# Splitting fp32 weights for TensorE in pairs of batches: one 1024-column split in place of two 512-column ones

## The chip, the core and the metric

One Trainium2 chip, one of its cores. The metric is the device time of one execution in microseconds (us), the median of several. All inputs are float32, and so is the output.

## What is computed

Two decoder blocks in a row over 256 tokens with model width 2048. Cut to what matters here:

```python
def first_block(x, ...):
    proj = rms_norm(x, g_mix_pre) @ w_in              # 2048 x 9728
    y_attn = sliding_window_attention(...)            # 16 heads of 64
    o = hgrn2_recurrence(...)                         # 8 heads of 128, a gated linear recurrence
    merged = sigmoid(gate_a) * (y_attn @ w_attn_branch) + sigmoid(gate_b) * (y_hgrn @ w_hgrn_branch)
    x = x + rms_norm(merged @ w_out)
    x = x + rms_norm((silu(gate) * up) @ w_down)      # gate, up = h @ w_gate_up, width 5632
    x = x + rms_norm((p @ w_ple_proj) * sigmoid(h @ w_ple_gate))

def second_block(x, ...):
    proj = rmsnorm(x) @ w_in_2
    o_a = dsa_mixer(...)                              # top-k index, latent attention, 8 heads
    o_b = fox_mixer(...)                              # forgetting attention, 8 heads
    x = x + concat(o_a, o_b) @ w_o
    x = x + conv_ffn(rmsnorm(x), w_up, conv_w, conv_b, w_down)
    return rmsnorm(x)
```

The weights, some 480 MB, are read once. Each product with a weight is made of three TensorE products of halves: a float32 number is split into a part `hi` that TensorE's fp32r format holds and a rest `lo`, and hi*hi + hi*lo + lo*hi is summed in PSUM.

## The kernel before, in words

The host packs the weights of all phases into units of 8 tiles of 128x128, so 128 partitions x 1024 columns, 512 KB. There are 902 units in one stream, in the order in which TensorE uses them. Half a unit, 4 tiles or 512 columns, is a batch; there are 1804, and a **tick** is the place of one batch in the program. All engines walk over the same ticks:

- **SyncE** (`fetch`, L2510) brings unit u into `raw`, a ring of 4 units (`RAW`), once the rest of unit u-4 has been taken (signal `rest`).
- **ScalarE (ACT)** (`half(b)`, L1071) casts batch b to `hi`, a ring of 6 batches (`SPL`). It waits until TensorE has finished batch b-6 (signal `gemm`, key "batch"), whose slot it takes.
- **VectorE (DVE)** (`low_half(b)`, L1637) subtracts: `lo` = `raw` - `hi`, in a ring of 6 too. It waits for `half(b)` (signal `halved`) and for the same batch of TensorE.
- **TensorE (PE)** (L609 to 1045) takes `hi` and `lo` of its batch, all through the helper `mm` at L613/614.

At tick t ACT and DVE split batch t+5 (`LOOK`). Beside that each engine has an `Agenda` (L311): a generator per piece of work (a group's epilogue, an attention head, a step of the recurrence) that names the ticks of its steps. Each engine executes strictly in the program's order. The loops of ACT (L1599) and DVE (L2431) are:

```python
for tick in range(plan.ticks):
    if tick in URGENT:
        agenda.run(tick)
    if tick + LOOK < plan.ticks:
        low_half(tick + LOOK)
```

From tick 48 on every tick is in `URGENT`, so the agenda of a tick comes ahead of the split made in it (ACT has three ticks as exceptions, `SPLIT_FIRST`). The agenda of tick t+1 comes behind it.

Groups come in two kinds. In the one the weight is what is loaded, and a batch is 4 matmuls of 512 columns with `hi` and 4 of 256 with `lo`. In a **quarter** (`batch_of_quarter`, L1011) the activations are loaded and the weights stream, 512 columns at a time, into two banks m = 0 and 1: six matmuls a batch. In the last three batches of a quarter (`SKEW`) TensorE does m=0 for all three first, and m=1 for all three after it, and a batch is finished for `gemm` only with m=1. So those three batches end one behind the other, about 2 us later than their m=0 halves.

The places outside the stream that matter for the prediction:

- **The ladder of the recurrence** (`hgrn`, PE L746, ACT L1463, DVE L2213), once for each of two sets of heads, from tick HG = 121 and from tick 193 (L588). It has 9 stages n = 0 to 8, four ticks apart (`LEVEL`). `product(n)` on DVE stands at tick HG+1+4n (n from 2 on), the copy of the keys (L1471) on ACT at HG+2+4n (n = 1 to 7), the matmuls `sums(n)` on PE at HG+4+4n, and `place(n)` on DVE at HG+6+4n (L604 to 606). `product(n+1)` needs `sums(n)`; the keys' copy needs `product`; `sums` need both.
- Its end: PE transposes at `HG_TURN` and `HG_TURN`+2 (L807, ticks 275 and 277), ACT and DVE make `HS` from the first at tick 276 (L1495, L1630), and the second pair of transposes needs those banks.
- **Latent attention** (`latent`, L851, L1506, L2341), two chains of four heads, 14 ticks a head, the one at odd ticks and the other at even ones, and **forgetting attention** (`forget`, L883, L1528, L2366), four chains of two heads. ACT lays the transposed probabilities (L1520, L1542) shortly ahead of the product that needs them.
- The crossings between phases (`CROSS`, L538): PE transposes `X` chunk by chunk (L653), ACT and DVE make `XS` from it, and the first batches of the next phase need it.

Of the kernel before, what the change touches and what calls it, by code (L numbers as in the profile page):

```python
# [8 lines left out]
F32 = mybir.dt.float32  # L9
# [3 lines left out]
ALU = mybir.AluOpType  # L13
# [11 lines left out]
RAW = 4  # L25
BT = 4
BW = BT * P
SPL = 6
LOOK = 5

PIECES = [(0, 1), (1, 2)] + [(c, c + 2) for c in range(2, 16, 2)]
# [297 lines left out]
def program(nc, d, out):  # L329
# [4 lines left out]
    with ctx:  # L334
        def sb(name, shape, dt=F32):
            return ctx.enter_context(nc.sbuf_tensor(name, shape, dt))
# [3 lines left out]
        def signal(name, step=1):  # L340
            signals.append(Signal(ctx.enter_context(nc.semaphore(name)), step))
            return signals[-1]

        raw = sb("raw", [P, RAW, UW])
        hi = sb("hi", [P, SPL, BW], F32R)
        lo = sb("lo", [P, SPL, BW], F32R)
        X = sb("X", [P, NC, T])
# [30 lines left out]
        def const(name, a=0, b=None, rows=slice(0, P)):  # L378
            lo_, hi_ = CCOL[name]
            return cst[rows, lo_ + a:(hi_ if b is None else lo_ + b)]  # L380
# [12 lines left out]
        def sums_of(n):  # L393
            a = 12 * BY_TOKEN.index(n) + 8
            return cols[:, a:a + 2]
# [4 lines left out]

        def cut(q, n=QUARTER):
            return slice(n * q, n * q + n)

        ident = const("ident")
        ones = const("ones", 0, P)
# [88 lines left out]
        halved, rest, gemm = signal("halved"), signal("rest"), signal("gemm")  # L494
# [114 lines left out]
        def tensor(eng, counting=False):  # L609
# [3 lines left out]
            def mm(o, l, r, start, stop):  # L613
                return eng.matmul(o, l, r, start=start, stop=stop, skip_group_check=True)  # L614

            def clear(k):
                for signal_key in free.get(k, ()):
                    on.wait_ge(*signal_key)
# [332 lines left out]
            def high(b, pos, g, j):  # L951

                w = hi[:, b % SPL, pos * P:(pos + 1) * P]
                if j == 0:
# [11 lines left out]
            def low_part(b, pos, g, j):  # L966

                w = lo[:, b % SPL, pos * P:(pos + 1) * P]
                o = bank[g.bank]
# [18 lines left out]
            def with_high(g, k, b, m):  # L988
# [4 lines left out]
                if k == 0:  # L993
                    clear(g.banks[m])
                o, w = bank[g.banks[m]], hi[:, b % SPL, :]
                mm(o, x[:, m * P:(m + 1) * P], w, k == 0, False)
                mm(o, x[:, T + m * P:T + (m + 1) * P], w, False, False)

            def with_low(g, k, b, m):

                x = operand(g, g.tiles[BT * k][2])[0]
                last = k == g.n // BT - 1
                t = mm(bank[g.banks[m]], x[:, m * P:(m + 1) * P], lo[:, b % SPL, :], False, last)
                done = [("batch", b)] if m else []
# [63 lines left out]
        def scalar(eng, counting=False):  # L1068
            on, agenda = On(eng, counting), Agenda()

            def half(b):  # L1071
                u, part = b // (UT // BT), b % (UT // BT)
                on.wait_ge(*((in_raw[u % RAW], u) if b else (in_first, 0)))
                if b >= SPL:
                    on.wait_ge(gemm, ("batch", b - SPL))
                eng.copy(hi[:, b % SPL, :], raw[:, u % RAW, part * BW:(part + 1) * BW]).then_inc(halved.next(b), 1)  # L1076
# [41 lines left out]
            def quarter_of_values(g):  # L1118

                n = ROOT_OF[g.kind]  # L1120
                if g.kind == "hi":
                    o = hh[g.q]["v"].rearrange("p (t n) -> p t n", t=2)
                else:
                    on.wait_ge(i_dve, "sel")
                    o = b_bv[:, :, cut(g.q)]
                on.wait_ge(n_dve, (n, "root"))
                for m in range(2):
                    if m:
                        yield 1
                    on.wait_ge(gemm, ("half", g.g, m))  # L1130
                    eng.activation(o[:, m, :], bank[g.banks[m]], ACT.Identity, scale=roots_of(n)[:, m:m + 1]).then_inc(
                        t_act.next((g.g, m)), 1)
# [17 lines left out]
            def quarter_of_gates(g):  # L1150

                o = {"ga": XT, "hg": h_gate[g.q % 2], "gb": gated}[g.kind]
                if g.kind == "gb":
                    on.wait_ge(h_pe, (0, "turned", 1))
                elif g.kind == "hg":
                    on.wait_ge(h_dve, (g.q, "product", 2))
                on.wait_ge(n_dve, ("mix", "root"))
                for m in range(2):
                    if m:
                        yield 1  # L1160
                    on.wait_ge(gemm, ("half", g.g, m))
                    eng.activation(o[:, m, :] if g.kind == "hg" else o[:, m, cut(g.q)], bank[g.banks[m]], ACT.Sigmoid, scale=roots_of("mix")[:, m:m + 1]).then_inc(
                        t_act.next((g.g, m)), 1)
# [35 lines left out]
            def quarter_of_down1(g):  # L1199
                q, p = g.i  # L1200
                if g is by["down1", (3, 2)]:
                    return
                for m in range(2):
                    if m:
                        yield 1
                    if p == 0:
                        on.wait_ge(gemm, ("half", g.g, m))
                        eng.copy(Y[:, m, cut(q)], bank[g.banks[m]]).then_inc(t_act.next((g.g, m)), 1)
                    elif p == 2:
                        square_of_down(g, m)  # L1210
# [376 lines left out]
            def enter_first(c):  # L1587
                on.wait_ge(in_x[piece_of(c)], 0)
                eng.activation(XS[:, c, 0:T], X[:, c, :], ACT.Identity, scale=col("g_mix_pre", c)).then_inc(
                    upper.next(("mix", c)), 1)  # L1590
# [4 lines left out]
            eng.activation(sums_of("final"), prm[:, 0:2], ACT.Identity).then_inc(n_act.next("first table"), 1)  # L1595
            for b in range(LOOK):
                enter_first(b)
                half(b)
            for tick in range(plan.ticks):  # L1599
                first = tick in URGENT and tick not in SPLIT_FIRST  # L1600
                if first:
                    agenda.run(tick)
                if tick + LOOK < plan.ticks:
                    half(tick + LOOK)
                if tick + LOOK < NC:
                    enter_first(tick + LOOK)
                if tick == NORM_AT["mix"]:
# [15 lines left out]
        def vector(eng, counting=False):  # L1623
            on, agenda = On(eng, counting), Agenda()

            def tt(o, a, b, op):
                return eng.tensor_tensor(o, a, b, op)  # L1627
# [9 lines left out]
            def low_half(b):  # L1637
                u, part = b // (UT // BT), b % (UT // BT)
                on.wait_ge(halved, b)
                if b >= SPL:  # L1640
                    on.wait_ge(gemm, ("batch", b - SPL))
                tt(lo[:, b % SPL, :], raw[:, u % RAW, part * BW:(part + 1) * BW], hi[:, b % SPL, :].bitcast(F32),
                   ALU.subtract).then_inc(rest.next(b), 1)
# [779 lines left out]
            def enter_first(c):  # L2423
                lower(XS[:, c, :], X[:, c, :], ("mix", c), col("g_mix_pre", c))

            eng.memset(HS[:, 0, :].bitcast(F32), 0.0).then_inc(zeros.next(0), 1)
            on.wait_ge(in_pre, 0)
            for b in range(LOOK):
                enter_first(b)
                low_half(b)  # L2430
# [281 lines left out]
```

## Time and profile before

| | |
|---|---|
| median of 3 runs | 2654.79 us (2652.17 to 2655.65) |
| span of the profiled execution | 2653.3 us |
| its busy time, PE | 2636.2 us, 99% |
| its busy time, PE loading weights | 2236.2 us, 84% |
| its busy time, DVE | 1871.7 us, 71% |
| its busy time, ACT | 1510.4 us, 57% |
| weights and inputs read | 488.44 MB, 186 GB/s |

For the profiled execution only its span is given, from its first to its last instruction; it lies 1.5 us under the median of the runs, inside their spread. Engines are named as in the profile: PE is TensorE's matmuls, PEld its weight loads, DVE VectorE, ACT ScalarE, POOL GpSimd, SP SyncE. Times inside the profile count from the span's start. A matmul's end in it is modelled, and matmuls overlap in their tails, as do neighbouring instructions of ACT and DVE by up to 0.1 us.

### The profile page before, as it was taken

What the parts mean: (1) busy time and instruction counts of PE and PEld (TensorE: products, weight loads), DVE (VectorE), ACT (ScalarE), POOL (GpSimd) and SP (SyncE); (2) the same over time, 40 slices, a digit from 0 to 9 for tenths busy, and PEclk for the clock granted to TensorE, in tenths of its full rate; (3) what the DMA queues carried; (4) which work ended last, traced back from release to release, by engine and by line L of the source; (5) the groups of instructions that cost most, each with busy time, mean ns of one, the idle gap of its engine ahead of it and who ended that gap; (6) DMA issues with size and microseconds to landing.
All of it is one profiled execution on the core that took longest, in us unless ns stands there. A gap on an engine that the chain in (4) does not pass through costs nothing.

```text
span 2653.3 us, 38713 instructions
## 1 busy us (share of the span) xinstructions
PE 2636.2 (99%) x13730; PEld 2236.2 (84%) x13730; DVE 1871.7 (71%) x3539; ACT 1510.4 (57%) x3006; POOL 38.8 (1%) x56
## 2 busy tenths in 40 slices
PE   9999999999999999999999999999999999999998
PEld 7888888888888888888887888988888888888887
DVE  7877566465876577657767678666688758866885
ACT  7775555455655455545557665554566546655654
POOL 0000000000000000000003000000000000000000
PEclk9999999999999999999999999999999999999999
DMA  8455547666666666665665555545656666666565
GB/s 282 147 167 162 181 152 238 192 208 197 184 187 191 206 204 187 193 191 186 188 188 178 173 161 187 156 149 162 186 180 192 193 192 186 190 190 192 187 192 160
DMA packets 136817, 493.09 MB, mean 186 GB/s; under 512 B 15704, under 2 KB 16216, under 8 KB 135856
## 3 DMA queue, kind: packets, MB, share of 16 engines
q1 hardware_dynamic: 134064, 480.04, 57.8%
q0 software_dynamic: 2272, 10.31, 1.2%
q8 instruction: 109, 1.79, 0.3%
q14 instruction: 84, 0.69, 0.1%
q10 hardware_dynamic: 288, 0.26, 0.0%
HBM read 488.44 MB, written 4.21 MB: 186 GB/s over the span
## 4 chain that ended last, share of the span: by engine, by line
PE 98%; DVE 1%; ACT 0%; issue 0%; DMA 0%; DVEq 0%; SPq 0%; ACTq 0%
PE bank L614 97%; PE bank L653 0%; DVE lo L1627 0%; DVE X L1630 0%; PE bank L729 0%; DVE arena L1627 0%; DVE XS L1630 0%; DMA raw<-in_ws_mix 0%; ACT sq_t L1181 0%; PE bank L867 0%; PE bank L901 0%; ACT hi L1076 0%; PE bank L677 0%; PE bank L694 0%; PE bank L807 0%
## 5 line engine op out<-in xcount | busy, mean ns | idle before, releaser
L1627 DVE TENSOR_TENSOR lo<-raw,hi 128x512 fp32r<-128x512 f32 x1804 | 1233.2, 690 | 659.7 <-ACT hi L1076 548.2
L1076 ACT CAST hi<-raw 128x512 fp32r<-128x512 f32 x1804 | 1098.0, 619 | 696.8 <-PE bank L614 678.1
L614 PE MATMUL bank<-XS,hi 128*128 128x512 f32 x3632 | 1000.2, 396 | 1.6 <-DVE XS L1630 1.6
L614 PEld LDWEIGHTS bank<-XS,hi 128*128 128x128 f32 x3632 | 620.8, 189 | 90.8 <-issue 4.0
L614 PEld LDWEIGHTS bank<-XS,lo 128*128 128x128 f32 x3632 | 557.0, 189 | 77.1
L614 PE MATMUL bank<-XS,lo 128*128 128x256 f32 x3632 | 578.5, 281 | 0.0
L614 PE MATMUL bank<-hi,HS 128*128 128x512 f32 x1952 | 545.6, 391 | 0.0
L614 PE MATMUL bank<-hi,XS 128*128 128x512 f32 x1600 | 448.3, 394 | 1.7 <-DVE XS L1630 1.1
L614 PEld LDWEIGHTS bank<-hi,HS 128*128 128x128 f32 x1952 | 364.0, 188 | 75.5 <-ACT hi L1076 1.3
L614 PEld LDWEIGHTS bank<-hi,XS 128*128 128x128 f32 x1600 | 296.8, 189 | 66.0 <-ACT hi L1076 4.4
L614 PE MATMUL bank<-lo,HS 128*128 128x512 f32 x976 | 321.6, 389 | 0.0
L614 PE MATMUL bank<-lo,XS 128*128 128x512 f32 x800 | 259.4, 390 | 0.0
L614 PEld LDWEIGHTS bank<-lo,HS 128*128 128x128 f32 x976 | 183.2, 188 | 38.8 <-DVE lo L1627 0.4
L614 PEld LDWEIGHTS bank<-lo,XS 128*128 128x128 f32 x800 | 150.5, 188 | 32.0
L1082 ACT COPY tmp_t<-bank 128x256 f32<-128x256 f32 x235 | 86.6, 373 | 143.7 <-PE bank L614 143.5
L1627 DVE TENSOR_TENSOR u_t<-bank,tmp_t 128x256 f32<-128x256 f32 x208 | 87.7, 423 | 51.2 <-ACT tmp_t L1082 50.9
L1630 DVE SCALAR_TENSOR_TENSOR u_t<-u_t,prm 128x255 f32<-128x255 f32 (+1 forms) x176 | 84.8, 483 | 9.0
L1627 DVE TENSOR_TENSOR u_t<-u_t,r_t 128x256 f32<-128x256 f32 x200 | 84.8, 424 | 6.8
L614 PE MATMUL bank<-arena 128*128 128x128 f32 (+4 forms) x672 | 87.4, 299 | 0.0
L614 PEld LDWEIGHTS bank<-arena 128*128 128x128 f32 (+2 forms) x672 | 71.7, 182 | 8.6 <-issue 2.4
L1285 ACT ACTIVATE u_t<-u_t,prm 128x256 f32<-128x256 f32 x88 | 53.0, 602 | 44.8 <-DVE u_t L1627 44.8
L1627 DVE TENSOR_TENSOR u_t<-u_t 128x256 f32<-128x256 f32 x178 | 75.3, 423 | 2.6 <-ACT u_t L1148 0.8
(198 smaller groups left out, 985.5 us busy)
## 6 DMA issues: line engine op xcount, KB each, us to landing
raw<-in_ws_ffn SPq DMA_DIRECT2D x528, 512.0 KB, 3.5
raw<-in_ws_mix SPq DMA_DIRECT2D x338, 512.0 KB, 3.6
raw<-in_ws_ple SPq DMA_DIRECT2D x35, 512.0 KB, 4.1
arena<-in_gains POOLq DMA_DIRECT2D x4, 1024.0 KB, 5.9
X<-in_xt POOLq DMA_DIRECT2D x1, 2048.0 KB, 13.1
t5rows<-t5row POOLq DMA_DIRECT2D x8, 256.0 KB, 5.1
out<-arena SPq DMA_DIRECT2D x8, 256.0 KB, 2.5
X<-in_x SPq DMA_DIRECT2D x7, 256.0 KB, 5.3
```

Source lines behind the costliest of these rows:

```text
L614: return eng.matmul(o, l, r, start=start, stop=stop, skip_group_check=True)
L1076: eng.copy(hi[:, b % SPL, :], raw[:, u % RAW, part * BW:(part + 1) * BW]).then_inc(halved.next(b), 1)
L1082: eng.copy(low(g), bank[g.bank][:, T:2 * T]).then_inc(copied.next(g.g), 1)
L1285: eng.activation(v, tile(g.u[0]), ACT.Identity, scale=col("cw", 176 + j), bias=col("cb", j)).then_inc(curved.next((g.g, "v")), 1)
L1627: return eng.tensor_tensor(o, a, b, op)
L1630: return eng.scalar_tensor_tensor(out=o, in0=a, scalar=s, in1=b, op0=op0, op1=op1)
```

## The change

From batch 8 on the two batches of a unit are split by one instruction on ACT and one on DVE, of 1024 columns instead of 512, into two neighbouring slots of the rings. That happens where the even one of the two had its turn; where the odd one had, nothing is left. The wait is the later one of the two: for batch b+1-6 = b-5, since the second of the two slots is written as well. Both batches get the same count of `halved` and of `rest`, so a waiter that has seen the even one waits no more for the odd one. The size of the rings, the order of TensorE and all agendas stay.

```diff
@@ -26,6 +26,7 @@
 SPL = 6
+PAIRED = 8
 LOOK = 5
@@ -401,6 +402,9 @@
+        def pair_of(ring, b):
+            return ring[:, b % SPL:b % SPL + 2, :].rearrange("p b n -> p (b n)")
+
@@ -1071,6 +1075,11 @@
             def half(b):
                 u, part = b // (UT // BT), b % (UT // BT)
                 on.wait_ge(*((in_raw[u % RAW], u) if b else (in_first, 0)))
+                if b >= PAIRED:
+                    if part == 0:
+                        on.wait_ge(gemm, ("batch", b + 1 - SPL))
+                        eng.copy(pair_of(hi, b), raw[:, u % RAW, :]).then_inc(halved.next(b, b + 1), 1)
+                    return
                 if b >= SPL:
                     on.wait_ge(gemm, ("batch", b - SPL))
@@ -1637,6 +1646,12 @@
             def low_half(b):
                 u, part = b // (UT // BT), b % (UT // BT)
                 on.wait_ge(halved, b)
+                if b >= PAIRED:
+                    if part == 0:
+                        on.wait_ge(gemm, ("batch", b + 1 - SPL))
+                        tt(pair_of(lo, b), raw[:, u % RAW, :], pair_of(hi, b).bitcast(F32), ALU.subtract).then_inc(
+                            rest.next(b, b + 1), 1)
+                    return
                 if b >= SPL:
                     on.wait_ge(gemm, ("batch", b - SPL))
```

How the order moves, at two places. The first is DVE in the second ladder, from `place(3)` at tick 211 over `product(5)` (the five `arena<-arena`, tick 214) to `place(4)` at tick 215. Before:

```order
L2268 COPY_PREDICATED arena<-lvl,bank 128x4x16x4 x2
L1627 TENSOR_TENSOR lo<-raw,hi 128x512 x3
L1627 TENSOR_TENSOR arena<-arena 128x4x8x8 x4
L1627 TENSOR_TENSOR arena<-arena 128x64
L1627 TENSOR_TENSOR lo<-raw,hi 128x512
L1627 TENSOR_TENSOR X<-X,bank 128x512
L2268 COPY_PREDICATED arena<-lvl,bank 128x4x8x8 x2
```

With the change (its lines are numbered higher, and `lo` is 1024 wide):

```order
L2283 COPY_PREDICATED arena<-lvl,bank 128x4x16x4 x2
L1636 TENSOR_TENSOR lo<-raw,hi 128x1024 x2
L1636 TENSOR_TENSOR arena<-arena 128x4x8x8 x4
L1636 TENSOR_TENSOR arena<-arena 128x64
L1636 TENSOR_TENSOR X<-X,bank 128x512
L2283 COPY_PREDICATED arena<-lvl,bank 128x4x8x8 x2
```

Ahead of the product there stood the subtraction of batch 218, which waits for batch 212; now there stands that of 218 and 219, which waits for batch 213. The subtraction that stood behind the product is gone.

The second place is ACT in the same ladder, from the keys of `sums(4)` (tick 211) over those of `sums(5)` (tick 215) to those of `sums(6)` (tick 219). Before:

```order
L1471 COPY arena<-arena 128x32x8 x2
L1076 CAST hi<-raw 128x512 x4
L1471 COPY arena<-arena 128x16x16 x2
L1076 CAST hi<-raw 128x512 x4
L1471 COPY arena<-arena 128x8x32 x2
```

With the change:

```order
L1480 COPY arena<-arena 128x32x8 x2
L1081 CAST hi<-raw 128x1024 x2
L1480 COPY arena<-arena 128x16x16 x2
L1081 CAST hi<-raw 128x1024 x2
L1480 COPY arena<-arena 128x8x32 x2
```

The four casts of batches 216 to 219 had four ticks for their turns, 211 to 214; the two wide ones stand at ticks 211 and 213, and the second waits for batch 213. Nothing stands any more between it and the keys of tick 215.

## Rows read from the trace of the kernel before

**Rows 1.** The page: span; busy time, share and instructions of each engine.

```profile
span 2653.3 us, 38713 instructions
...
PE 2636.2 (99%) x13730; PEld 2236.2 (84%) x13730; DVE 1871.7 (71%) x3539; ACT 1510.4 (57%) x3006; POOL 38.8 (1%) x56
```

**Rows 2.** Groups by form: count, busy us, mean ns, idle before and its releasers.

```profile
L1627 DVE TENSOR_TENSOR lo<-raw,hi 128x512 fp32r<-128x512 f32 x1804 | 1233.2, 690 | 659.7 <-ACT hi L1076 548.2 <-PE bank L614 96.9
L1076 ACT CAST hi<-raw 128x512 fp32r<-128x512 f32 x1804 | 1098.0, 619 | 696.8 <-PE bank L614 678.1 <-DMA raw<-in_ws_mix 13.2 <-issue 0.3
...
L1276 ACT CAST HS<-u_t 128x256 fp32r<-128x256 f32 x44 | 18.0, 408 | 60.2 <-DVE u_t L1627 60.2
...
L1627 DVE TENSOR_TENSOR arena<-arena 128x1024 f32<-128x1024 f32 x2 | 2.4, 1218 | 0.0
```

**Rows 3.** All waits: engine, line, releaser: us in total, times, longest.

```profile
PEld bank L614 <- ACT hi L1076: 9.1, 18, 1.1
```

**Rows 4.** Timeline, one batch after another in a plain stretch: start, us, instruction.

```profile
1000.55 1.09 PE L614 MATMUL bank<-XS,hi 128*128 128x512 f32 x4
...
1001.96 1.09 PE L614 MATMUL bank<-XS,hi 128*128 128x512 f32 x4
```

**Rows 5.** Timeline, second ladder, ticks 209 to 213.

```profile
336.16 1.06 PE L614 MATMUL bank<-arena 128*128 128x128 f32 x8
...
338.30 1.62 DVE L1627 TENSOR_TENSOR arena<-arena 128x256 f32<-128x256 f32 x5
...
338.64 0.62 ACT L1076 CAST hi<-raw 128x512 fp32r<-128x512 f32 x1 [1.06 <-PE bank L614]
...
339.96 0.71 ACT L1471 COPY arena<-arena 128x256 f32<-128x256 f32 x2 [0.70 <-DVE arena L1627]
...
342.55 1.06 PE L614 MATMUL bank<-arena 128*128 128x128 f32 x8
```

**Rows 6.** Timeline, the same ladder at a quarter's end, ticks 213 to 217.

```profile
344.06 1.56 DVE L1627 TENSOR_TENSOR arena<-arena 128x256 f32<-128x256 f32 x5
...
346.39 0.62 ACT L1076 CAST hi<-raw 128x512 fp32r<-128x512 f32 x1 [2.97 <-PE bank L614]
...
346.91 0.71 ACT L1471 COPY arena<-arena 128x256 f32<-128x256 f32 x2
...
348.92 1.06 PE L614 MATMUL bank<-arena 128*128 128x128 f32 x8
```

**Rows 7.** Timeline, the ladder's end, ticks 276 and 277.

```profile
436.66 1.40 DVE L1630 SCALAR_TENSOR_TENSOR HS<-bank,prm,HS 128x512 fp32r<-128x512 f32 x2
...
437.31 0.63 ACT L1076 CAST hi<-raw 128x512 fp32r<-128x512 f32 x1 [0.41 <-PE bank L614]
...
438.47 1.03 PE L807 MATMUL bank<-cst,arena 128*128 128x128 f32 x8
```

**Rows 8.** Timeline, one head of latent attention at even ticks.

```profile
1718.02 0.37 ACT L1082 COPY tmp_t<-bank 128x256 f32<-128x256 f32 x1 [1.05 <-PE bank L614]
...
1718.29 0.49 ACT L1520 COPY arena<-bank 128x384 f32<-128x384 f32 x1
...
1719.22 0.83 PE L614 MATMUL bank<-arena 128*128 128x128 f32 x6
```

**Rows 9.** Timeline, forgetting attention.

```profile
1782.69 0.88 ACT L1542 COPY arena<-bank 128x384 f32<-128x384 f32 x2
...
1784.09 0.61 PE L614 MATMUL bank<-arena 128*128 128x128 f32 x4
```

**Rows 10.** Timeline, a crossing behind a quarter of `o1`, ahead of the second feed-forward network.

```profile
1874.36 0.39 PE L614 MATMUL bank<-lo,HS 128*128 128x512 f32 x1
...
1875.89 0.68 DVE L1627 TENSOR_TENSOR X<-X,bank 128x512 f32<-128x512 f32 x1
...
1877.31 0.38 PE L653 MATMUL bank<-cst,X 128*128 128x128 f32 x2
```

**Rows 11.** The page: DMA issues, count, KB each, us from issue to landing.

```profile
raw<-in_ws_ffn SPq DMA_DIRECT2D x528, 512.0 KB, 3.5
```

## Prediction

> **What bounds the kernel now.** First the page's busy times: of a span of 2653.3 us PE is busy 2636.2, and only 17.1 are left [rows 1]. So the bound is TensorE, and an edit can take away at most those 17.1 us unless it makes PE do less. This one doesn't: order and number of its 13730 matmuls stay. Then the groups: the two splits are the largest work of ACT (1098.0 us) and DVE (1233.2), but both engines stand idle in front of them, ACT for 678.1 us until PE gives a slot free, DVE for 548.2 us until ACT has cast [rows 2]. They are ahead and wait. Then the waits: PE's loads waited for `hi` 9.1 us in all, in 18 places [rows 3]. Faster splits can return little more than that. What the change can cost is read from the other side, the chains in which PE waits for a step of ACT or DVE that stands in the same queue as the splits, and for those I read the timeline.
>
> **What it removes.** From batch 8 on 1796 batches become 898 pairs. On DVE two of 690 ns become one of 1218 ns, which the trace has in another place [rows 2]. On ACT no cast of 1024 columns is there; 256 columns take 408 ns and 512 take 619 [rows 2], so 211 ns more for 256 columns, and 619 + 2 x 211 = 1041 ns. Two casts of 619 bound it from above (1.24 us); from below I have no nearer row than the slope itself, and the price of a single cast, 0.62, as the extreme. I take 1.04. So DVE saves 162 ns and ACT 197 ns a pair, 145 and 177 us in all, on engines that are 71% and 57% busy, ahead of PE and waiting. On the path this is worth about nothing; it hides behind PE's matmuls and would count only where the splits are late, in the 9.1 us of rows 3. The 2 x 898 waits that PE no longer has to make are worth nothing either: batches follow each other every 1.41 us [rows 4] with both waits in them. Nothing in these rows tells a satisfied wait from none; were it 10 ns, 1796 would be 18 us, which is the gain's outer bound and more than PE's idle time.
>
> The Trainium skill, page "Perfetto Trace Analysis", section "Optimizing Scalar/DVE Operations", says that grouping into larger operations helps if the engine is saturated, and that where these engines aren't saturated but cause bubbles on others, breaking instructions up may let work be done sooner. By that rule this change goes the wrong way; rows 2, with hundreds of microseconds of idle time ahead of the splits, are the second case.
>
> **What it adds: later splits.** Before, batch b could be split once batch b-6 was done, five batches or 7.0 us ahead of its use, and was ready 0.62 + 0.69 us after that; 5.7 us were left. Now the even batch of a pair starts one batch later, 5.6 us ahead, and needs 1.04 + 1.22 = 2.26; 3.4 us are left. That covers the splits themselves nearly everywhere. The fetch of a unit waits for the second subtraction as before, whose slot is the same; it comes 2.26 - 1.31 = 0.95 us later, of about 11 us (eight batches) between slot and next use, with a landing of 3.5 us [rows 11]. Nothing.
>
> **What it moves: every step at an even tick.** The wide split stands at odd tick t and waits for the end of batch t itself, not t-1. All that ACT has at tick t+1 now starts no earlier than 1.04 us after batch t, and all that DVE has there 2.29 us after it (cast, 0.03 to pass on, subtraction). Before, ACT's was free at the end of batch t-1 plus 0.62. Behind that waiting instruction the agenda of the even tick is queued, and PE waits for it where its slack is smaller. Place by place:
>
> - *The ladders.* `product` is at an even tick in both (HG = 121 and 193, +1+4n). At tick 209 the cast that waits for batch 209 starts at 338.64; the product then already runs on DVE, from 338.30, and the keys are done at 340.67, 1.9 us ahead of the sums at 342.55 [rows 5]. Now: cast 338.64 to 339.68, subtraction 339.71 to 340.93, product (1.62, of which 0.1 overlaps) to 342.45, keys (0.71) to 343.2. The sums come 0.65 us late. Of the steps with keys behind a `sums` (`product` 2 to 7, six a ladder, 12 in all) four have their odd tick at the third last batch of a quarter, whose end is put off behind the m=0 halves: ticks 141, 205, 213, 221. There the cast waits until 346.39 [rows 6]: then cast to 347.43, subtraction to 348.68, product (1.56) to 350.15, keys to 350.9, against sums at 348.92, 2.0 us late. The delay comes again in each step, since the gate is counted from PE's own progress: 8 x 0.65 + 4 x 2.0 = **13.2 us**. `product(8)` needs no keys and comes just in time.
> - *The ladder's end.* Cast 437.31 to 438.35, subtraction to 439.60, then the two `HS` of 1.40 to 441.0; PE wants their banks at 438.47 and half a microsecond later [rows 7]: **2.0 us**. It happens once, with the banks of the first set of heads.
> - *Latent attention.* The chain at even ticks has four heads. ACT's copies begin when the batch is done, 1718.02, and end at 1718.78, 0.44 us ahead of PE at 1719.22 [rows 8]. Behind a wide cast they end 1.05 later: 0.6 us, four times, **2.4 us**.
> - *Forgetting attention.* The same at two places with 0.52 us of slack (1783.57 to 1784.09) [rows 9]: 2 x 0.5 = **1.0 us**.
> - *Crossings behind `o1`.* The quarter's last batch ends at 1874.75; cast to 1875.82, subtraction to 1877.05, the addition at the even tick (0.68) to 1877.7, against 1877.31 [rows 10]: 0.4 us in each of four quarters, **1.6 us**.
> - *Where splits were late already.* The start, the second half of `wa`, and the three phase changes with chains of DVE: even batches come up to 0.95 us later there. I take one such delay for each of these five, **5 us**. This is an estimate from the 0.95, without a row of its own; zero and 10 us are its ends.
>
> Sum: 13.2 + 2.0 + 2.4 + 1.0 + 1.6 + 5 = 25.2 us. Against the span of 2653.3 that is 2678.5; the median of the runs lies 1.5 us higher than the profiled span, so **2680 us**. With a wide cast of 1.24 us each of the some 30 places would be 0.2 later, 6 us more.
>
> **The rivals.** (1) *The rings absorb it*: the cast or DVE's queue is not what holds the products, or my place of the gate is off, and PE's stalls stay under 0.2%, which is 5.3 us and about what a measurement of this kernel can tell from no change. For it: 3.4 us stay in hand nearly everywhere. Against it: the ladder's chain has its own slack of 1.9 us, not the ring's. Time: 2655 (2650 to 2660). Chance 0.10. (2) *Faster*, the other side: the splits that PE waited for become 0.2 us a pair shorter on ACT and 0.16 on DVE, and where ACT is behind by several batches the queue drains sooner. It decides from the point at which those savings outweigh the waits for the later slot, so if most of the 9.1 us of rows 3 are ACT's backlog and the ladders stay in time. It gives back at most 9.1, likely half: 2650. Chance 0.05. The skill's first clause, on grouping, is this case. (3) *The delays chain*: a late product delays DVE's `place` and the next subtraction, the keys delay the next wide cast, and PE's stalls in ladder and attention double, or its clock falls in one of them: 25 x 2 = 50 us, 2705. For it: DVE is at 71% on average and more in the ladder. Chance 0.12. (4) The change does what it says; the order shows the moved instructions, so I give that no chance of its own.
>
> **How the numbers follow.** The forecast, slower by 6 to 42 us, has 0.73. Its own range: the ladders alone at half price give 2662, all places at full price with a 1.24 us cast and 10 us for the late splits 2692; knock-on between them brings it to 2698. The range that holds 8 in 10 leaves out rivals 1 and 2 and the larger part of 3: 2662 to 2700. Faster by over 0.2% only in rival 2, 0.05; within 0.2% rival 1, 0.10; slower 0.85.
>
> **What would show it.** Right: DVE `lo` at 1.22 us and ACT `hi` at 1.04, 898 of each; PE's idle time up from 17 to some 42 us, half of it ahead of the `arena` matmuls of L614 in the two ladders, in stalls of 0.6 and of 2 us with ACT L1471's copy as releaser; some 2 us at L807; the matmuls' own durations unchanged. Wrong: sums in time with the keys done ahead of them, PE's new idle time in front of `hi` and `lo` of plain batches (then the ring is the bound and not the ladder), or a shorter batch than 1.41 us, which would mean that a wait cost PE something.

## The result, and the profile after

The changed kernel takes **2717.97 us** (median of 4 runs, 2712.19 to 2720.03), the kernel before beside it on the same chip 2654.67 (4 runs). The ratio is 1.0234, with a 95% interval of 1.0221 to 1.0246: slower by 63.3 us in the medians and by 61.7 us in the profiled spans (2715.0 against 2653.3), some 62 us below. The forecast was 2680 in a range of 2662 to 2700. Direction and kind of loss were right, its size was not. One of the 11 runs of `plain_only` below took 2884.18 us at a mean granted clock of 0.849 of 2.4 GHz, where the others on record had 0.994 to 0.999, and is left out of its comparison.

First the page of the changed kernel: span, and busy time, share and instructions of each engine; then the two split groups (count, busy us and mean ns, idle before and its releasers). Line numbers are those of each kernel's own file: L1636, L1081, L1480, L618 here are L1627, L1076, L1471, L614 of the kernel before. `arena` is a shared area of SBUF in which several phases keep their tiles.

```profile
span 2715.0 us, 35753 instructions
...
PE 2656.9 (98%) x13730; PEld 2239.8 (82%) x13730; DVE 1765.1 (65%) x2641; ACT 1368.5 (50%) x2108; POOL 40.9 (2%) x56
...
L1636 DVE TENSOR_TENSOR lo<-raw,hi 128x1024 fp32r<-128x1024 f32 x898 | 1099.7, 1226 | 811.8 <-ACT hi L1081 796.8 <-PE bank L618 11.2
...
L1081 ACT CAST hi<-raw 128x1024 fp32r<-128x1024 f32 x898 | 937.5, 1046 | 801.0 <-PE bank L618 794.6 <-DMA raw<-in_ws_mix 5.3
```

Against [rows 1, 2]: the wide splits cost what they were put at, 1226 and 1046 ns. ACT does 142 us less and DVE 107 us less than before, a fifth to a quarter less than the 177 and 145 that the prediction counted, and both stand idle longer ahead of the splits. PE's idle time is 2715.0 - 2656.9 = 58.1 us, where it was 17.1; the other 20.7 us are in its busy time, and come back below.

What PE's matmuls wait for, from all waits of the changed kernel (engine, line, releaser: us in total, times, longest):

```profile
PE bank L618 <- ACT arena L1480: 13.9, 11, 2.2
PE bank L657 <- DVE X L1639: 7.5, 4, 3.2
PE bank L618 <- DVE X L1636: 3.3, 5, 1.0
PE bank L618 <- DVE XS L1639: 3.0, 6, 0.7
PE bank L618 <- ACT hi L1081: 2.6, 4, 1.1
PE bank L657 <- DVE X L1636: 2.4, 3, 0.8
PE bank L681 <- DVE arena L1636: 2.2, 3, 0.8
PE bank L811 <- DVE HS L1639: 1.8, 1, 1.8
PE bank L618 <- ACT arena L1121: 1.7, 1, 1.7
```

And, of what its weight loads wait for, the splits:

```profile
PEld bank L618 <- DVE lo L1636: 6.5, 12, 1.2
...
PEld bank L618 <- ACT hi L1081: 4.7, 7, 1.6
```

The largest is the one that the prediction named: the ladders' sums (L618) behind the keys (ACT L1480), 11 stalls. The others are spread over steps of many kinds, `X`, `XS`, `HS`, and copies of the attention. The splits themselves hold PE a little more than before: its loads wait for `lo` 6.5 us, for `hi` 4.7 and for the eight narrow casts at the start 2.3, together 13.5, against 9.5 before (9.1 of [rows 3] and 0.4 for `lo`); its matmuls, which the loads overlap, wait 5.0 us for them against 0.4. To see every place, not only waits that have a releaser, I paired each matmul of PE with the same one of the kernel before, whose order is the same, and took by how much its start had moved at the ends of each stretch. The table gives these growths in us; a gain is negative, the columns behind `after` are the experiments below, and a dash is no row of the forecast.

| place | forecast | after | odd_turn | ladder_only | no_ladder | narrow_early | act_only |
|---|---|---|---|---|---|---|---|
| start and first attention | part of 5 | 12.6 | -0.1 | 1.3 | 12.4 | 7.4 | 7.5 |
| two ladders | 13.2 | 20.0 | 0.2 | 22.3 | 0 | 6.1 | 11.4 |
| second half of `wa` | part of 5 | 1.7 | 3.4 | 0 | 1.7 | 0.4 | 1.4 |
| ladder's end | 2.0 | 2.7 | 0 | 0 | 2.2 | 1.2 | 1.7 |
| merges of heads | - | 4.4 | 0 | 0 | 3.3 | 0 | 1.4 |
| four phase changes | part of 5 | 11.5 | 11.5 | 1.4 | 11.2 | 2.7 | 7.8 |
| keys and values, latent attention | 2.4 | 4.9 | 0.8 | 0 | 4.8 | 0.6 | 3.3 |
| forgetting attention | 1.0 | 0.4 | -1.5 | -1.7 | 0.3 | -1.7 | 0 |
| crossings behind `o1` | 1.6 | 4.0 | 1.1 | 0 | 4.0 | 0 | 2.7 |
| second feed-forward network | 0 | 0.0 | 18.4 | 0 | 0 | 0 | 0 |
| sum | 25.2 | 61.8 | 33.7 | 23.3 | 40.0 | 16.9 | 37.1 |

(What is missing to a sum lies in small steps between the places. The forecast's 5 us counted three phase changes, of the four that there are. Of the 4.4 us at the merges in `after`, 1.1 lie with a fall of the clock at 475.7, told below, and not with a stall.) One ladder step in the timeline of the changed kernel, a product whose odd tick is a quarter's third last batch; its sums are those that start at 336.16 in [rows 5] (start, us, instruction, in brackets the idle time before and its releaser):

```profile
356.75 1.05 ACT L1081 CAST hi<-raw 128x1024 fp32r<-128x1024 f32 x1 [3.21 <-PE bank L618]
...
357.83 1.23 DVE L1636 TENSOR_TENSOR lo<-raw,hi 128x1024 fp32r<-128x1024 f32 x1 [3.03 <-ACT hi L1081]
...
358.97 1.76 DVE L1636 TENSOR_TENSOR arena<-arena 128x256 f32<-128x256 f32 x5
...
360.76 0.71 ACT L1480 COPY arena<-arena 128x256 f32<-128x256 f32 x2 [2.38 <-DVE arena L1636]
...
361.61 1.13 PE L618 MATMUL bank<-arena 128*128 128x128 f32 x8 [2.24 <-ACT arena L1480]
```

Here stand the links that the prediction drew out of [rows 5, 6]: ACT and DVE each idle 3 us in front of a split whose slot isn't free, then cast, subtraction, product, keys, one behind the other, and PE waits 2.24 us at the sums. In [rows 6], a place of the same kind, the keys were done at 347.62, 1.3 us ahead of the sums.

The place that the prediction had no line for is the first attention. Before, where ACT's copy L1112 is the last thing PE waits for:

```profile
61.88 0.58 ACT L1112 COPY arena<-bank 128x512 f32<-128x512 f32 x1
...
62.55 0.93 PE L614 MATMUL bank<-arena 64*128 64x128 f32 x8
```

And in the changed kernel:

```profile
66.17 1.04 ACT L1081 CAST hi<-raw 128x1024 fp32r<-128x1024 f32 x1 [1.20 <-PE bank L618]
...
67.12 0.58 ACT L1121 COPY arena<-bank 128x512 f32<-128x512 f32 x1
...
67.75 0.93 PE L618 MATMUL bank<-arena 64*128 64x128 f32 x8 [1.68 <-ACT arena L1121]
```

Before, the copy ended at 62.46 and PE followed at 62.55, with 0.09 us in hand. Whatever stands ahead of that copy in ACT's queue shows at PE nearly in full. In this stretch there are 14 stalls of over 0.35 us, which sum to 10.2. In one of them, of 1.3 us at 146.53, PE waits for a cast itself; but that cast stood behind steps of ACT of which the first had waited 3.62 us for DVE, whose steps stood behind a wide subtraction.

### The profile page after: what moved, and what is told of

The parts are those of the page before. It is cut to its first block, busy times and chain, and to the rows that moved or that the text cites. A ratio compares the mean times of both kernels' runs of the same rounds, so it can differ in the third digit from the quotient of the medians.

```text
span 2715.0 us, 35753 instructions
## 1 busy us (share of the span) xinstructions
PE 2656.9 (98%) x13730; PEld 2239.8 (82%) x13730; DVE 1765.1 (65%) x2641; ACT 1368.5 (50%) x2108; POOL 40.9 (2%) x56
## 3 DMA queue, kind: packets, MB, share of 16 engines
q8 instruction: 109, 1.79, 0.3%
## 4 chain that ended last, share of the span: by engine, by line
PE 87%; DVE 6%; ACT 4%; issue 2%; DMA 1%; ACTq 0%; SPq 0%; DVEq 0%
PE bank L618 86%; ACT hi L1081 2%; DVE lo L1636 2%; DVE arena L1636 1%; PE bank L657 1%; DMA raw<-in_ws_mix 1%; DVE u_t L1636 0%; DVE arena L1639 0%; DVE X L1636 0%; ACT arena L1459 0%; ACT sq_t L1190 0%; DVE X L1639 0%; ACT arena L1480 0%; DVE arena L1643 0%; DVE XS L1639 0%
## 5 line engine op out<-in xcount | busy, mean ns | idle before, releaser
L1636 DVE TENSOR_TENSOR lo<-raw,hi 128x1024 fp32r<-128x1024 f32 (+1 forms) x906 | 1105.1, 1221 | 814.2 <-ACT hi L1081 796.8
L1081 ACT CAST hi<-raw 128x1024 fp32r<-128x1024 f32 x898 | 937.5, 1046 | 801.0 <-PE bank L618 794.6
L618 PE MATMUL bank<-XS,hi 128*128 128x512 f32 x3632 | 1001.0, 397 | 3.1 <-DVE XS L1639 1.2
L618 PEld LDWEIGHTS bank<-XS,hi 128*128 128x128 f32 x3632 | 621.4, 189 | 92.5 <-issue 6.0
L618 PEld LDWEIGHTS bank<-XS,lo 128*128 128x128 f32 x3632 | 556.7, 189 | 80.7 <-DVE lo L1636 3.7
L618 PE MATMUL bank<-XS,lo 128*128 128x256 f32 x3632 | 579.4, 281 | 1.1 <-DVE lo L1636 0.9
L618 PE MATMUL bank<-hi,HS 128*128 128x512 f32 x1952 | 548.2, 392 | 0.7 <-ACT hi L1081 0.7
L618 PE MATMUL bank<-hi,XS 128*128 128x512 f32 x1600 | 449.5, 395 | 3.9 <-DVE XS L1639 1.8
L618 PEld LDWEIGHTS bank<-hi,HS 128*128 128x128 f32 x1952 | 365.5, 189 | 76.7 <-ACT hi L1081 1.4
L618 PEld LDWEIGHTS bank<-hi,XS 128*128 128x128 f32 x1600 | 297.2, 189 | 69.4 <-issue 5.3
L618 PE MATMUL bank<-lo,HS 128*128 128x512 f32 x976 | 322.9, 391 | 0.6 <-DVE lo L1636 0.5
L618 PE MATMUL bank<-lo,XS 128*128 128x512 f32 x800 | 259.8, 391 | 0.1
L618 PEld LDWEIGHTS bank<-lo,HS 128*128 128x128 f32 x976 | 184.1, 189 | 40.1 <-DVE lo L1636 1.5
L618 PEld LDWEIGHTS bank<-lo,XS 128*128 128x128 f32 x800 | 150.4, 188 | 33.2 <-DVE lo L1636 1.3
L1639 DVE SCALAR_TENSOR_TENSOR u_t<-u_t,prm 128x255 f32<-128x255 f32 (+1 forms) x176 | 84.9, 483 | 59.5 <-ACT u_t L1294 56.4
L618 PE MATMUL bank<-arena 128*128 128x128 f32 (+4 forms) x672 | 89.8, 303 | 19.6 <-ACT arena L1480 13.9
L618 PEld LDWEIGHTS bank<-arena 128*128 128x128 f32 (+2 forms) x672 | 71.2, 184 | 33.8 <-DVE arena L1636 11.9
L1636 DVE TENSOR_TENSOR u_t<-u_t 128x256 f32<-128x256 f32 x178 | 75.4, 424 | 30.1 <-ACT u_t L1157 23.9
L1636 DVE TENSOR_TENSOR u_t<-u_t,r_t 128x256 f32<-128x256 f32 x200 | 85.0, 425 | 6.7
L1636 DVE TENSOR_TENSOR u_t<-bank,tmp_t 128x256 f32<-128x256 f32 x208 | 86.6, 417 | 0.0
```

What stands on the lines that cost most here:

```text
L1081: eng.copy(pair_of(hi, b), raw[:, u % RAW, :]).then_inc(halved.next(b, b + 1), 1)
L1639: return eng.scalar_tensor_tensor(out=o, in0=a, scalar=s, in1=b, op0=op0, op1=op1)
```

## The experiments

Two theories. **A**: the loss is in the queues. A wide split waits in front of steps that PE needs, and they run after it. **B**: the loss is in the rings. The splits of plain batches come too late for PE, because a pair is begun later and takes longer. I name the runs as their texts do; B there is in some of them a cost of each pair, spread evenly over the run. The kernel before took 2655.65 us (median of 7 runs) beside the first four experiments and 2655.22 (21 runs) beside the others; differences are against these. Code is shown in part.

### odd_turn: the same wide splits, at the odd batch's turn

The wait is for the same batch, but the split now stands one tick later, behind the agenda of the even tick instead of ahead of it.

```diff
                 if b >= PAIRED:
-                    if part == 0:
-                        on.wait_ge(gemm, ("batch", b + 1 - SPL))
-                        eng.copy(pair_of(hi, b), raw[:, u % RAW, :]).then_inc(halved.next(b, b + 1), 1)
+                    if part == 1:
+                        on.wait_ge(gemm, ("batch", b - SPL))
+                        eng.copy(pair_of(hi, b - 1), raw[:, u % RAW, :]).then_inc(halved.next(b - 1, b), 1)
                     return
```

(and the same in `low_half`; the waits for `raw` and for `halved` stand at the odd turn too.)

> The same 898 wide splits with the same gate (pair (b-1, b) waits for batch b-6), but standing at the odd batch's turn, one tick later in the program: behind the agenda of the even tick instead of ahead of it. Theory A (what costs is the queue: the even tick's steps stand behind an instruction that waits for the batch of its own tick): the steps at even ticks are free again, PE's stalls in the two ladders fall from 16 us to under 3, and the whole comes to 2655 to 2668 us. Theory B (the ring is what costs: even batches are split one batch later and 1.04 + 1.22 us long, whatever the order): gate and width are unchanged, so the time stays near 2715.

Measured: 2687.72 us (2686.44 to 2688.83), ratio 1.0121 [1.0105, 1.0136]. About half of the loss is gone, which neither theory had. The table says why. In start and attention, ladders, ladder's end, merges, and keys, values and latent attention the growth falls from 44.6 us to 0.9, with splits just as wide and the same slots to wait for: for these places A is shown. But the phase changes lose 11.5 us again (how, comes below), and the second feed-forward network, which had lost nothing, now loses 18.4. Its waits in 2100 to 2500 us of this kernel:

```profile
ACT u_t L1295 <- DVE u_t L1637: 38.5, 38, 1.2
ACT HS L1307 <- DVE u_t L1637: 38.2, 20, 2.0
ACT u_t L1301 <- DVE u_t L1640: 31.9, 21, 1.7
PEld bank L618 <- DVE lo L1637: 11.6, 25, 0.5
```

And of the kernel before in the same stretch, where the list has no wait of PE for `lo`:

```profile
ACT HS L1297 <- DVE u_t L1627: 21.4, 21, 1.0
ACT u_t L1285 <- DVE u_t L1627: 18.6, 43, 0.4
ACT u_t L1291 <- DVE u_t L1630: 13.7, 22, 0.6
```

ACT's own steps on `u_t` wait for DVE, whose steps stand behind wide subtractions. The cast at the odd turn stands behind those waiting steps, as in this piece of `odd_turn`'s timeline:

```profile
2202.04 1.23 DVE L1637 TENSOR_TENSOR lo<-raw,hi 128x1024 fp32r<-128x1024 f32 x1
...
2204.27 0.42 ACT L1301 ACTIVATE u_t<-u_t 128x256 f32<-128x256 f32 x1 [1.66 <-DVE u_t L1640]
...
2204.59 1.03 ACT L1082 CAST hi<-raw 128x1024 fp32r<-128x1024 f32 x1
```

and the subtraction reaches PE late: 25 waits of its loads in this stretch, none over 0.5 us. PE's late splits are what B names, but what makes them late is again the queue, whose order puts the split last. So one order hurts the steps, the other the splits.

### ladder_only and no_ladder: where the loss lies

Both take the change's own form, in `ladder_only` only where the even turn lies in the ticks of the two ladders, in `no_ladder` everywhere else (there the test is `not any(...)`); this is `ladder_only`'s edit:

```diff
+LADDERS = [(121, 160), (193, 232)]
+
+
+def paired(b):
+    turn = b - b % 2 - LOOK
+    return b >= PAIRED and any(x <= turn < y for x, y in LADDERS)
...
-                if b >= PAIRED:
+                if paired(b):
```

> Pairs only where their turn lies in one of the two ladders (ticks 121 to 159 and 193 to 231), narrow splits elsewhere: 78 of 1804 ticks. Theory A (PE stalls at chains with little slack): the ladder's 11 stalls of 0.8 to 2.4 us come back in full, +15.7 us and a little in small ones, 2668 to 2674. Theory B (a cost per pair, spread over the run): 4% of the loss of 63 us, +3, 2658.

> The complement: pairs everywhere but in the two ladders. Theory A: 63 - 17 = +46 us, 2701, and PE's stalls ahead of the arena matmuls fed by the keys' copy are gone. If the stalls of the different places hide one another, more than that: 2705 to 2715. Theory B: +60, 2715.

Measured: `ladder_only` 2677.08 us (2675.12 to 2678.47), ratio 1.0078 [1.0062, 1.0095]; `no_ladder` 2694.9 (2693.03 to 2697.4), 1.0148 [1.0133, 1.0164]. That is 21.4 and 39.2 us, together 60.6: the ladders and the rest add up, and don't feed each other. 78 ticks of 1804 hold a third of the loss, at the sums, as PE's waits in `ladder_only` show:

```profile
PE bank L624 <- ACT arena L1486: 14.5, 12, 2.2
```

A cost spread evenly over the pairs, B in that run's text with 2658, falls as the cause of that third. But two thirds lie outside the ladders, where the forecast had 12 us.

### narrow_early: both splits at the even turn, but narrow

```diff
-                        on.wait_ge(gemm, ("batch", b + 1 - SPL))
-                        eng.copy(pair_of(hi, b), raw[:, u % RAW, :]).then_inc(halved.next(b, b + 1), 1)
+                        for k in range(2):
+                            on.wait_ge(gemm, ("batch", b + k - SPL))
+                            eng.copy(hi[:, (b + k) % SPL, :], raw[:, u % RAW, k * BW:(k + 1) * BW]).then_inc(halved.next(b + k), 1)
```

(and the same in `low_half`, which waits for each batch's `halved` too.)

> The order of the change with instructions of the old width: both batches of a pair are split at the even one's turn, each by its own 512-column cast and subtraction with its own gate (b-6, then b-5). Steps at even ticks now wait for the own tick's batch, but for 0.62 + 0.69 = 1.3 us behind it and not 2.3. Theory A: an ordinary step of the ladder is 0.3 us in time again, the four at a quarter's end are 1.0 us late, other places lose 0.4 (ACT) or 0.95 us (DVE) less each: in all +15 to +25 us, 2670 to 2680. If the width is what costs: no change against before, 2655. If the order is all: near 2715.

Measured: 2672.94 us (2671.84 to 2675.04), ratio 1.0066 [1.0051, 1.0081]; 17.3 us. The queues' order and the last wait are those of the change; what is left behind that wait is 0.62 and 0.69 us instead of 1.05 and 1.23. The same ladder place as above in its timeline:

```profile
344.39 1.76 DVE L1637 TENSOR_TENSOR arena<-arena 128x256 f32<-128x256 f32 x5
...
346.19 0.71 ACT L1481 COPY arena<-arena 128x256 f32<-128x256 f32 x2 [1.85 <-DVE arena L1637]
...
347.04 1.13 PE L618 MATMUL bank<-arena 128*128 128x128 f32 x8 [1.23 <-ACT arena L1481]
```

A stall of 1.23 us where the wide split made 2.24, though the two narrow subtractions together take longer than the wide one. So of the 62 us some 17 come with the moved wait alone, and 45 are that after it the whole pair has to be done before anything behind it.

### act_only: wide on ACT alone

The block `if b >= PAIRED` in `low_half` is taken out, and DVE subtracts batch by batch as before.

> ACT's cast wide at the even turn as in the change, DVE's subtractions narrow in their own turns. Theory A: the product of the ladder starts 0.53 us earlier, behind a subtraction of 0.69 instead of 1.22, so ordinary steps are 0.1 to 0.6 us late instead of 0.8 to 1.3 and those at a quarter's end 1.5; steps of ACT at even ticks lose the full 1.05 us. In all +30 to +45 us, 2685 to 2700. If DVE's width were the whole cost: 2655 to 2665; if ACT's were: 2715.

Measured: 2692.5 us (2690.91 to 2693.02), ratio 1.0139 [1.0126, 1.0153]; 37.3 us. ACT's wide cast alone makes 37 of the 62 us, and DVE's wide subtraction on top of it the other 25: a step passes through both queues. The subtraction wide by itself was not run, so 25 is its part behind a wide cast only. In the ladders, whose chain runs over DVE, act_only has 11.4 of 20 us.

### plain_only and hybrid: wide where no step is near

`turn_of` gives the turn of the pair, even (0), odd (1), or None for narrow ones. For `plain_only` the list holds only the two feed-forward networks; for `hybrid` it adds the other stretches and takes the odd turn everywhere but in the last:

```diff
+WIDE = [(0, 236, 1), (256, 425, 1), (470, 950, 1), (1070, 1235, 1), (1330, 1804, 0)]
+
+
+def turn_of(b):
+    even = b - b % 2 - LOOK
+    if b < PAIRED:
+        return None
+    return next((part for x, y, part in WIDE if x <= even < y), None)
```

with `[(470, 950, 0), (1330, 1804, 0)]` in `plain_only`.

> Pairs as in the change, but only in the plain stretches of the two feed-forward networks (turns at ticks 470 to 949 and 1330 to 1803): 477 of 898 pairs, none at a chain that PE waits for. Theory A (the cost sits in chains with little slack, and the saved time of ACT and DVE buys nothing): 2655, within 0.1% of before, though ACT's and DVE's busy time falls by some 90 us each. A cost per pair: 477/898 of 62 us, +33. A gain per pair from shorter instructions: below 2650.

> Pairs in 85% of the ticks, each stretch in the order that left PE alone there: at the odd batch's turn in the attention, ladders, merges and the heads of the second block, at the even one's turn in the second feed-forward network, narrow splits at the phase changes and at wa. Theory A (order and slack of each place, additive): 2652 to 2657, the loss of 62 us gone with 763 pairs still there. If pairs cost something by themselves that order doesn't mend, or if odd and even turns disturb each other: over 2665.

Measured: `plain_only` 2654.48 us (2653.15 to 2655.71), ratio 0.9997 [0.9988, 1.0006]; `hybrid` 2655.08 (2653.2 to 2657.18), 0.9999 [0.999, 1.0007]. Hybrid's page:

```profile
span 2652.0 us, 36198 instructions
...
PE 2636.7 (99%) x13730; PEld 2236.2 (84%) x13730; DVE 1786.8 (67%) x2782; ACT 1396.2 (53%) x2249; POOL 38.7 (1%) x56
```

757 pairs are split wide (its text said 763), ACT does 114 us and DVE 85 us less than in [rows 1], and the time doesn't move. The ladder step of [rows 5] in it:

```profile
337.81 1.63 DVE L1646 TENSOR_TENSOR arena<-arena 128x256 f32<-128x256 f32 x5
...
337.87 1.05 ACT L1091 CAST hi<-raw 128x1024 fp32r<-128x1024 f32 x1 [1.23 <-PE bank L626]
...
339.35 1.22 DVE L1646 TENSOR_TENSOR lo<-raw,hi 128x1024 fp32r<-128x1024 f32 x1
339.47 0.72 ACT L1490 COPY arena<-arena 128x256 f32<-128x256 f32 x2 [0.55 <-DVE arena L1646]
...
341.72 1.06 PE L626 MATMUL bank<-arena 128*128 128x128 f32 x8
```

The product comes first and the split after it; the keys end at 340.19, 1.5 us ahead of the sums, near the 1.9 of before. So the wide split gains nothing that shows, to 0.1%, also where it does no harm. (Its times at this place stand 0.8 us earlier than in [rows 5], which it has from its first 51 us.) No version here beats the kernel before.

### ladder_warm: what the clock has of it

The records of the granted clock fall to the lower level several times in the changed kernel. Windows of it around these (window, its us, busy us with count of PE, PEld, DVE, ACT, POOL, granted clock as a share of 2.4 GHz, DMA share, GB/s):

```profile
257.00:261.00 4.00, 3.79 (x14) 3.39 (x15) 1.23 (x1) 1.60 (x3) 0.00 (x0) 0.57 0.33 95
363.00:367.00 4.00, 4.00 (x12) 3.14 (x12) 1.61 (x2) 1.05 (x2) 0.00 (x0) 0.57 0.36 131
475.00:479.00 4.00, 4.00 (x16) 3.08 (x14) 0.30 (x1) 0.20 (x1) 0.00 (x0) 0.59 0.35 131
1448.00:1456.00 8.00, 6.75 (x20) 5.34 (x21) 6.98 (x13) 5.86 (x10) 7.19 (x7) 0.57 0.23 67
```

The second comes right behind the stall at 361.61 shown above: PE is busy through it, at 1.2 GHz. The first four and a fifth at 1554.3 sum to 20.5 us; in the kernel before there was one of 3.4 us, at 1798.8 (a last one behind PE's last matmul stands in every run and costs nothing). Paired with the same matmuls of the kernel before, those in the five kept PE busy 8.6 us longer, and the one before costs 1.6 us, near half of its 3.4. `ladder_warm` is `ladder_only` with three matmuls more ahead of the product's wait, into a bank that is about to be overwritten, in steps 2 to 7 of both ladders: 36 that add nothing to the result. The wait for that bank (`clear`), which stood behind the product's, moves ahead of them:

```diff
+                    clear(pair[0])
+                    if 2 <= n < len(STAGES) - 1:
+                        for _ in range(3):
+                            mm(bank[pair[0]], XS[:, 0, 0:P], XS[:, 0, :], True, True)
                     if m:
                         on.wait_ge(h_dve, (f, "product", n))
```

> ladder_only (2677.1) with three matmuls of 512 columns into the bank that the sums will overwrite, ahead of PE's wait in steps 2 to 7 of each ladder, 36 in all: they add nothing to the result and fit (0.68 us) into stalls of 0.5 to 2.2 us. In ladder_only the granted clock fell to 1.2 GHz three times in the second ladder, 3.4 us each. If that is a part of the loss (5.2 of its 21 us): the clock stays at 2.4 GHz in the ladder and the time falls to 2671 to 2673. If the clock costs nothing there or falls all the same: 2677 to 2679, the fillers that don't fit on top.

Measured: 2674.21 us (2670.88 to 2674.68), ratio 1.0068 [1.0052, 1.0083]; 19.0 us over its own kernel before where `ladder_only` had 21.4, though the two intervals overlap; the time alone doesn't show it, the traces do. The second ladder in both, `ladder_only` first:

```profile
325.00:400.00 75.00, 66.38 (x306) 54.51 (x305) 44.60 (x75) 25.47 (x36) 0.00 (x0) 0.93 0.41 132
```

```profile
325.00:400.00 75.00, 70.19 (x352) 58.02 (x352) 45.02 (x77) 28.00 (x47) 0.00 (x0) 1.00 0.43 142
```

The granted clock stays whole, and the second ladder grows by 10.2 us instead of 14.8, while the first, in which neither has a fall, grows by 7.6 and 7.5: the three falls of 3.4 us that `ladder_only` has there cost 4.6 us, near half of their 10.2. The filling work takes the idle time of stalls that were there anyway. The stalls themselves remain, and so does the larger part of the loss.

## Why the prediction was right and wrong

- **What it removes: right.** Splits of 1226 and 1046 ns against 1218 and 1041; their savings, 142 and 107 us instead of 177 and 145, hidden behind PE. That a satisfied wait costs nothing was left with an outer bound of 18 us. In `hybrid` 225 pairs, with 450 waits fewer, lie between 760 and 1400 us, where PE has no stall: its starts there moved by 0.001 us in all. Over the whole run the interval of the ratio leaves at most 0.1%, 2.7 us.
- **The ladders: right in mechanism, place and releaser, too small.** "8 x 0.65 + 4 x 2.0", 13.2 us, met 20.0. Eleven stalls over 0.35 us sum to 15.7 (PE's starts against before). The four at quarter ends are of 1.93 to 2.40 us and sum to 8.7, against 8.0. The ordinary ones are seven of 0.77 to 1.34 and sum to 7.0, against 5.2 for eight. The term took every product at [rows 5]'s 1.62 us, and the largest two, of 1.34, stand behind products of 2.03 us; and it let the sums start as the keys end, where 0.14 us lie between (361.47 and 361.61 above). The eighth, which is the very step of [rows 5] from which 0.65 was worked out, made no stall:

```profile
368.87 0.71 ACT L1480 COPY arena<-arena 128x256 f32<-128x256 f32 x2 [2.83 <-DVE arena L1636]
...
369.73 1.13 PE L618 MATMUL bank<-arena 128*128 128x128 f32 x8
```

  The clock had fallen at 363.1, PE's own batches before these sums took longer (8.12 us from sums to sums, 6.39 before), and the keys were done at 369.58, 0.15 us ahead. So that fall stands partly in place of a stall. Of the other 4.3 us the two falls of the clock, at 257 and 363, make 3.4.
- **The ladder's end 2.0, latent 2.4, forgetting 1.0.** The end measured 2.7, 1.9 of it at L811. Latent's four stalls, at the copy that was named, were of 0.34 to 0.61 us and made 1.9; the 4.9 of the table hold also 2.5 ahead of them, at keys and values, which had no term. Forgetting measured 0.4, but only with the gain of the clock fall that is no longer there; without it it is some 2 us, twice the forecast.
- **Crossings behind `o1`: 1.6 against 4.0.** Four stalls of 0.95 to 1.0 instead of 0.4. The step counted one wide subtraction ahead of the addition that PE waits for. In the trace of after the addition ahead of that one already comes behind a wide subtraction of its own, and both delays arrive: subtractions at 1928.87 and 1930.61 with the addition of 1930.01 between them, and only then the addition of 1931.75, behind which PE starts at 1932.57.
- **"Where splits were late already": the step that failed.** It put five places at 0.95 us each, "an estimate ... without a row of its own; zero and 10 us are its ends". What it stood for measured about 30 us: start and first attention 12.6, merges 4.4, phase changes 11.5, `wa` 1.7. So the step put 5 us where 30 were, 25 of the 36.6 us that the forecast is short. Two errors lie in it. It counted late splits, while start, attention and merges lose as the ladders do, by steps of ACT and DVE queued behind a split: `odd_turn` takes them to zero. And the search for places with little in hand left out the first attention and the merges, where it isn't one delay but many. Late splits, what the step did count, are `wa`'s part: two waits of 0.84 and 0.69 us. At the phase changes PE waits for DVE's `X` of L1639, 7.5 us in all and 3.2 at the longest, at 1449.25, where before it was 3.7. That `odd_turn` has 11.5 us there too is the sum coming out alike, not each place: the first grows by 3.5 us instead of 1.7, the second by 2.4 instead of 4.6. Of the third's 1.9 us in `after` 1.3 are the clock's. `narrow_early` brings the four down to 2.7 in all, so the length of the pair counts there as well; step by step these places were not taken apart, and their cause stays open in that part.
- **The clock was put in no term of the sum**, only in rival 3. It makes some 7 us (8.6 less 1.6), which lie within the places above, the phase changes above all. Rival 3 came nearest in time, 2705. Of its two mechanisms the falling clock did happen, at that price; delays that chain from place to place did not, since `ladder_only` and `no_ladder` add up to the whole. Within a place two delays do follow one another at the crossings, as told.
- **What would show it, and what would be wrong**: idle time "from 17 to some 42" was 58.1; half of it ahead of the `arena` matmuls was a quarter (13.9 of 58.1), since the rest was so much larger; L811 (before L807) had its 1.8. New idle time in front of `hi` and `lo`, the sign against the theory, came in small part: 4.6 us at the matmuls (5.0 against 0.4), of 41 in all. "The matmuls' own durations unchanged" holds at 2.4 GHz only. Of the 20.7 us by which PE's busy time grew 8.6 lie in the falls of the clock, and 11.9 in the first 16 matmuls behind each of the 56 places at which idle time grew: their first matmuls start 49.0 us late in sum for 41.6 us of new idle time, and groups behind a stall read longer (the sums 1.13 instead of 1.06 us). So a stall costs more than its idle time.
- **The Trainium skill**, page "Perfetto Trace Analysis", section "Optimizing Scalar/DVE Operations", says that where these engines aren't saturated but cause bubbles on other engines, breaking instructions up may let work be completed sooner. The runs agree: `narrow_early` is the change with its two instructions broken up again, at 17 us instead of 62.

A deeper ring, which would move the wait of the wide splits to an earlier batch, was not tried.

## What to carry to other kernels

A merged instruction takes the latest wait of its parts and holds its whole length ahead of everything queued behind it; its price is read at those steps, not at its own consumer. List every step of that engine on which the bound engine waits with less in hand than the new wait and length add, all phases and the short ones at the start too, before a sum is closed. Time saved on an engine that waits is worth nothing (here 114 and 85 us gave 0), so leave such an instruction narrow, or put it behind the steps of its turn, if those aren't waiting themselves: where they were, that order cost 18.4 us.

## What the runs showed of the hardware

- TensorE's granted clock fell to 1.2 GHz for 3.4 us (once 6.8) at stalls of 1.8 to 3.2 us, most of them between otherwise dense batches, in a kernel whose mean clock stays at 0.996. In `ladder_only` three such falls cost 4.6 us, about as much as two of the stalls behind which they come; matmuls into a bank about to be overwritten kept it at 2.4 GHz.
- A stall alone doesn't decide it. In the changed kernel the stalls of 2.04 and 1.99 us that end at 378.37 and 394.24 have no fall behind them. Those at 1798.8 in the kernel before and at 1784.9 in `ladder_warm` come with no idle time of PE over 0.2 us in the 12 us ahead; the one of before is gone in the changed kernel (1.6 us back). The kernel before, `ladder_only` and `hybrid` all have the same stall of 1.79 us (it ends at 1505.63, 1529.19 and 1504.81), and only in the two experiments a fall comes behind it. `narrow_early` has none while PE works.
- In a stretch without stalls (760 to 1400 us of `hybrid`) 450 satisfied waits fewer moved PE's starts by 0.001 us.
- Twice the width costs 1046 against 2 x 619 ns on ACT and 1226 against 2 x 690 ns on DVE.
